# One compact body per engine for the expert loop, with full tiles of 128 slots only

## The reference

```python
def moe_swiglu(h, w_router, w_gu, w_down):
    logits = (h @ w_router).astype(jnp.float32)
    top_vals, top_idx = lax.top_k(logits, TOP_K)          # TOP_K = 2
    gates = jax.nn.softmax(top_vals, axis=-1)
    comb = jnp.sum(jax.nn.one_hot(top_idx, N_EXPERTS, dtype=jnp.float32) * gates[..., None], axis=-2)
    y = jnp.zeros_like(h)
    for e in range(N_EXPERTS):                            # N_EXPERTS = 8
        y = y + comb[..., e:e + 1] * swiglu(h, w_gu[e], w_down[e])
    return y
```

## Time and profile before

| | before |
|---|---|
| median of 3 runs | 1827.52 us (1825.49 to 1830.34) |
| span of the profiled execution | 1824.5 us |
| PE busy | 1688.0 us (93%) |
| DVE busy | 1270.3 us (70%) |
| ACT busy | 1020.9 us (56%) |
| mean granted TensorE clock | 0.964 |
| HBM read | 449.06 MB |

### The profile page before, as it was taken

One profiled execution on the slowest core, in us unless ns is written; L12 is line 12 of the kernel. 1 busy time (PEld: TensorE's weight loads), 2 busy tenths in 40 slices (PEclk: granted clock), 3 DMA queues, 4 the chain that ended last, 5 costly groups with the idle time before them and its releaser, 6 DMA issues.

```text
span 1824.5 us, 21578 instructions
## 1 busy us (share of the span) xinstructions
PE 1688.0 (93%) x7605; PEld 1391.9 (76%) x7606; DVE 1270.3 (70%) x1081; ACT 1020.9 (56%) x883; POOL 9.6 (1%) x22
## 2 busy tenths in 40 slices
PE   7999999999997889979979979979998899799996
PEld 5887778887786778868868868868886688688785
DVE  6645644454697568868878878856654788788886
ACT  4344433433476367757757757644544577577674
POOL 0000000000000000000000000000000000000000
PEclk9999999999998799989989989989998999899999
DMA  9553455555421269979979979946665699799893
GB/s 350 193 199 111 143 189 194 185 192 180 167 96 44 79 230 370 348 252 369 350 254 369 349 255 374 333 164 228 223 215 177 222 378 340 257 368 349 318 367 135
DMA packets 191716, 452.27 MB, mean 248 GB/s; under 512 B 8492, under 2 KB 8892, under 8 KB 191420
## 3 DMA queue, kind: packets, MB, share of 16 engines
q1 hardware_dynamic: 189212, 445.35, 69.2%
q10 hardware_dynamic: 2336, 4.78, 0.7%
HBM read 449.06 MB, written 1.05 MB: 247 GB/s over the span
## 4 chain that ended last, share of the span: by engine, by line
PE 88%; DVE 7%; issue 3%; ACT 1%; DMA 0%; DVEq 0%; POOL 0%; SPq 0%; ACTq 0%; POOLq 0%
PE bank L1218 28%; PE bank L1219 28%; PE bank L1222 26%; DVE y L996 2%; DVE wlo L739 2%; PE bank L1374 2%; PE bank L1483 1%; PE bank L1484 1%; DMA raw<-in_ret_w_in 0%; DVE z L751 0%; PE bank L1464 0%; PE bank L1262 0%; ACT whi L414 0%; DVE res L1160 0%; PE bank L1442 0%
## 5 line engine op out<-in xcount | busy, mean ns | idle before, releaser
L739 DVE TENSOR_TENSOR wlo<-raw,whi 128x2048 fp32r<-128x2048 f32 x422 | 964.3, 2290 | 340.4 <-ACT whi L414 340.1
L414 ACT ACTIVATE whi<-raw 128x2048 fp32r<-128x2048 f32 x422 | 807.7, 1916 | 423.0 <-PE bank L1222 366.3
L1218 PE MATMUL bank<-whi,xh 128*128 128x512 f32 x1520 | 607.9, 400 | 83.4 <-issue 62.4
L1219 PE MATMUL bank<-wlo,xh 128*128 128x512 f32 x1520 | 601.0, 395 | 0.0
L1222 PE MATMUL bank<-whi,xl 128*128 128x512 f32 x1408 | 556.5, 395 | 0.0
L1218 PEld LDWEIGHTS bank<-whi,xh 128*128 128x128 f32 x1520 | 291.8, 192 | 146.6 <-issue 71.1
L1219 PEld LDWEIGHTS bank<-wlo,xh 128*128 128x128 f32 x1520 | 291.3, 192 | 59.1
L1222 PEld LDWEIGHTS bank<-whi,xl 128*128 128x128 f32 x1408 | 269.8, 192 | 57.7
L1218 PE MATMUL bank<-whi,hTh 128*128 128x512 f32 x616 | 242.3, 393 | 4.4 <-DVE hTl L921 2.5
L1219 PE MATMUL bank<-wlo,hTh 128*128 128x512 f32 x616 | 242.6, 394 | 0.0
L1222 PE MATMUL bank<-whi,hTl 128*128 128x512 f32 x560 | 218.6, 390 | 0.0
(11 more groups left out here) (184 smaller groups left out, 792.1 us busy)
## 6 DMA issues: line engine op xcount, KB each, us to landing
raw<-in_moe_w_gu SPq DMA_DIRECT2D x224, 1024.0 KB, 6.4
raw<-in_moe_w_down SPq DMA_DIRECT2D x112, 1024.0 KB, 6.6
raw<-in_ffn_w_gu SPq DMA_DIRECT2D x28, 1024.0 KB, 5.1
raw<-in_ret_w_in SPq DMA_DIRECT2D x24, 1024.0 KB, 6.0
raw<-in_ffn_w_down SPq DMA_DIRECT2D x14, 1024.0 KB, 4.9
raw<-in_conv_w_pw SPq DMA_DIRECT2D x12, 1024.0 KB, 5.0
raw<-in_ret_w_out SPq DMA_DIRECT2D x8, 1024.0 KB, 4.8
res<-in_x SPq DMA_DIRECT2D x2, 512.0 KB, 4.6
```

The costliest lines, as they stand in the source:

```text
L414: nc.scalar.activation(whi[base % SPLIT][:, :], raw[base % RAW][:, :], ACT.Copy).then_inc(hi_done, 1)
L739: nc.vector.tensor_tensor(wlo[base % SPLIT][:, :], raw[base % RAW][:, :], whi[base % SPLIT][:, :].bitcast(f32), ALU.subtract).then_inc(lo_ ...
L1218: nc.tensor.matmul(dst, ah, bh, start=start, stop=False)
L1219: last = nc.tensor.matmul(dst, ah, bl, start=False, stop=stop and al is None)
```

## The change

- `by_need` and its three variants go. On each engine one loop over all eight experts holds one branch: a count above 128 runs `expert(e, (FULL, FULL))` with 24 matmuls a block, all others `expert(e, (FULL,))` with 12. A kind HALF_FULL is defined and not used.
- The gather is per tile of 128 slots. Tile 0 of the next expert is gathered ahead of the last two down blocks; tile 1 at the start of a wide expert.
- The scatter of the previous expert comes after the next expert's two gate blocks. For expert 0 it scatters a column of `comb` that is zero; one more `y_hi`, `y_lo`, scatter and `accumulate` follow the loop. A wide expert scatters its second tile at its own end (`scatter(1, SCAT2)`, `accumulate2`) and PE waits for that.
- The up blocks of an expert's first step are followed by the index transposes, by matmuls with a zero matrix that open the DOWN banks (two, or four for a wide expert), and by the turn. `rows` of an expert then never starts a bank.
- `build_onehot` makes eight writes of 64 columns instead of six, right behind the first `hidden` of an expert. Slot tables take eight small operations instead of two and two.
- xh and xl, and hTh and hTl, lie interleaved in one buffer each. SP loads the blocks in plain order.

The core of the diff:

```diff
-        def by_need(eng, need, piece):
-            with eng.If(need > 0):
-                with eng.If(need > 1):
-                    piece(TWO)
-                with eng.Else():
-                    piece(PACKED)
-            with eng.Else():
-                piece(ONE)
...
# SP
+            with sp.Fori(0, NE) as e:
+                wg, wd = expert(moe_w_gu, e), expert(moe_w_down, e)
+                gu(wg, B_MOE, 0, STEPS * e)
                 with sp.Fori(0, STEPS - 1) as i:
-                    gu(wg, B_MOE + 4, i + 1, STEPS * j + i)
-                    down(wd, B_MOE + 8, i, STEPS * j + i)
+                    gu(wg, B_MOE + 4, i + 1, STEPS * e + i)
+                    down(wd, B_MOE + 8, i, STEPS * e + i)
+                down(wd, B_MOE + 40, STEPS - 1, STEPS * e)
...
# ACT
+            def expert(e, tiles):
+                six, done = STEPS * e, STEPS * e + STEPS
+                xh_gathered(e)
+                if tiles == 2:
+                    xh_gathered2(wide_before(act, e))
+                hi(B_MOE + 1, six)
+                y_hi(B_MOE + 6 * six)
+                hi(B_MOE + 2, six)
+                hi(B_MOE + 3, six)
+                silu(done, B_MOE + 2 + 6 * six, tiles)
+                hi(B_MOE + 4, six)
+                hi(B_MOE + 5, six)
+                ohT_evac(e, tiles)
+                with act.Fori(0, STEPS - 1) as i:
+                    hTh_evac(done + 1 + i, tiles)
+                    hi(B_MOE + 6, six + i)
+                    hi(B_MOE + 7, six + i)
+                    hi(B_MOE + 8, six + i)
+                    silu(done + 1 + i, B_MOE + 6 + 6 * (six + i), tiles)
+                    hi(B_MOE + 9, six + i)
+                    hi(B_MOE + 10, six + i)
+                    hi(B_MOE + 11, six + i)
+                hTh_evac(done + STEPS, tiles)
+                if tiles == 2:
+                    y_hi2(B_MOE + MOE_BLOCKS + 6 * six)
...
# DVE
             def build_onehot(e):
-                for i, (a, b) in enumerate(((0, P), (0, HALF), (HALF, P))):
-                    at_ = (0, P, P)[i]
-                    for t in range(TILES):
-                        last = nc.vector.tensor_scalar(onehot[:, t, at_ + a:at_ + b], iota[:, a:b],
-                                                       slot[:, i, t, bass.ds(e, 1)], None, ALU.is_equal)
+                for h in range(2):
+                    for n in range(2 * TILES):
+                        at_ = n % 2 * P + h * HALF
+                        last = nc.vector.tensor_scalar(onehot[:, n // 2, at_:at_ + HALF], iota[:, h * HALF:(h + 1) * HALF],
+                                                       slot[:, bass.ds(e, 1), n, h], None, ALU.is_equal)
                 last.then_inc(onehot_done, 1)
...
+            def expert(e, tiles):
+                six, done = STEPS * e, STEPS * e + STEPS
+                n2 = wide_before(dve, e) if tiles == 2 else None
+                xl_gathered(e, tiles, n2)
+                lo(B_MOE + 1, six)
+                y_lo(e)
+                lo(B_MOE + 2, six)
+                lo(B_MOE + 3, six)
+                accumulate(e)
+                hidden(done, B_MOE + 4 + 6 * six, tiles)
                 dve.wait_ge(ohT_ps, e + 1)
                 build_onehot(e + 1)
...
                 lo(B_MOE + 4, six)
                 lo(B_MOE + 5, six)
+                with dve.Fori(0, STEPS - 1) as i:
+                    hTl_evac(done + 1 + i, tiles)
+                    for b in range(6, 10):
+                        lo(B_MOE + b, six + i)
+                    hidden(done + 1 + i, B_MOE + 8 + 6 * (six + i), tiles)
+                    lo(B_MOE + 10, six + i)
+                    lo(B_MOE + 11, six + i)
+                hTl_evac(done + STEPS, tiles)
+                if tiles == 2:
+                    y_lo2(n2)
+                    accumulate2(e, n2)
...
# PE
+            def gather(e, tile):
+                for c in range(DC):
+                    dst = bank[2 * tile + c // 4][:, c % 4 * P:(c % 4 + 1) * P]
                     for t in range(TILES):
+                        where = onehot[:, t, tile * P:(tile + 1) * P]
+                        nc.tensor.matmul(dst, zh[:, t, c * P:(c + 1) * P], where, start=t == 0, stop=False)
+                        last = nc.tensor.matmul(dst, zl[:, t, c * P:(c + 1) * P], where, start=False, stop=t == TILES - 1)
+                return last
...
+            def expert(e, kinds):
+                six, done, tiles = STEPS * e, STEPS * e + STEPS, len(kinds)
+                gates = (FULL,) * tiles
+                n2 = wide_before(pe, e) if tiles == 2 else None
+                if tiles == 2:
+                    gather(e, 1).then_inc(gather2_ps, 1)
+                pe.wait_ge(xel_done, e + 1)
+                columns(B_MOE, bank[0:2], 0, kinds=gates, six=six)
+                columns(B_MOE + 1, bank[0:2], 1, kinds=gates, six=six)
+                pe.wait_ge(yl_done, e + 1)
+                scatter(0, SCAT).then_inc(scat_ps, 1)
+                pe.wait_ge(hTl_done, done)
+                columns(B_MOE + 2, bank[2:4], 0, kinds=kinds, six=six)
+                columns(B_MOE + 3, bank[2:4], 1, kinds=kinds, six=six)
+                pe.wait_ge(res_done, 2 * e + 8)
+                onehot_turn(tiles)
+                for n in range(2):
+                    nc.tensor.matmul(DOWN[0][n][:, :], zeros[:, 0:P], zeros[:, :], start=True, stop=False)
+                if tiles == 2:
+                    pe.wait_ge(ohT_done, e + 1)
+                    for n in range(2):
+                        nc.tensor.matmul(DOWN[1][n][:, :], zeros[:, 0:P], zeros[:, :], start=True, stop=False)
+                hT_turn(done, kinds)
+                with pe.Fori(0, STEPS - 1) as i:
+                    pe.wait_ge(silu_done, done + 1 + i)
+                    columns(B_MOE + 4, bank[0:2], 0, kinds=gates, six=six + i)
+                    columns(B_MOE + 5, bank[0:2], 1, kinds=gates, six=six + i)
+                    pe.wait_ge(hTl_done, done + 1 + i)
+                    columns(B_MOE + 6, bank[2:4], 0, kinds=kinds, six=six + i)
+                    columns(B_MOE + 7, bank[2:4], 1, kinds=kinds, six=six + i)
+                    expert_rows(B_MOE + 8, 0, False, kinds, six + i)
+                    expert_rows(B_MOE + 9, 2, False, kinds, six + i)
+                    hT_turn(done + 1 + i, kinds)
+                pe.wait_ge(silu_done, done + STEPS)
+                pe.wait_ge(onehot_done, e + 2)
+                gather(e, 0).then_inc(gather_ps, 1)
+                pe.wait_ge(hTl_done, done + STEPS)
+                expert_rows(B_MOE + 40, 0, False, kinds, six)
+                expert_rows(B_MOE + 41, 2, True, kinds, six)
+                if tiles == 2:
+                    pe.wait_ge(y2l_done, n2 + 1)
+                    scatter(1, SCAT2).then_inc(scat2_ps, 1)
+                    pe.wait_ge(acc2_done, n2 + 1)
...
+            with pe.Fori(0, NE) as e:
+                need = need_of(pe, e)
+                with pe.If(need > 1):
+                    expert(e, (FULL, FULL))
+                with pe.Else():
+                    expert(e, (FULL,))
+            pe.wait_ge(yl_done, NE + 1)
+            scatter(0, SCAT).then_inc(scat_ps, 1)
```

More of the change, by code:

```diff
@@ L501, in silu @@
                     act.wait_ge(hid_done, s)
[L502 to L507, removed]
+                for t in range(tiles):
+                    last = nc.scalar.activation(sgate[:, t, :], bank[t][:, :], ACT.Silu)
@@ L526, in step @@
[L526 to L531, removed]
+                for t in range(tiles):
+                    last = nc.scalar.activation(hTh[:, :, t, :],
+                                                bank[2 + t][:, :].rearrange("p (c n) -> p c n", c=4), ACT.Copy)
+                last.then_inc(hTh_done, 1)
+            def step(base, s, six):
+                hi(base, six)
+                hi(base + 1, six)
+                hTh_evac(s, TILES)
@@ L724, in _ @@
+            act.wait_ge(plan_done, 1)
+            with act.Fori(0, NE) as e:
+                need = need_of(act, e)
+                with act.If(need > 1):
+                    expert(e, 2)
+                with act.Else():
+                    expert(e, 1)
+                with act.If(e < NE - 1):
+                    hi(B_MOE + MOE_BLOCKS, STEPS * e)
+            y_hi(B_MOE + MOE_BLOCKS * NE)
             squares(4)
@@ L1212, in _ @@
+            y_lo(NE)
+            accumulate(NE)
             norm(4)
@@ L1512, in gates @@
-            def gates(base, need, e, s, six=0):
-                def piece(half, tiles):
-                    pe.wait_ge(silu_done, s)
-                    pe.wait_ge(xel_done, 2 * e + half + 1)
-                    columns(base + half, bank[0:2], half, tiles=tiles, six=six)
-                by_need(pe, need, lambda tiles: piece(0, tiles))
-                by_need(pe, need, lambda tiles: piece(1, tiles))
-            def ups(base, need, six=0):
-                for half in range(2):
```

(17 more changed lines are left out.)

535 lines of the change are left out of this document (191 added, 344 removed).

## The result

The changed kernel took 1837.57 us (median of 4 runs, 1835.4 to 1839.02) beside 1826.51 us of the kernel before: 1.0053 of its time, interval 1.0039 to 1.0068. It is slower by half a per cent. (With a fourth run, the median of the kernel before is 1826.51, where the three runs listed ahead had 1827.52.) The forecast was faster by 0.27%, so its sign was wrong, though the time lies inside the range, and just inside the 1810 to 1838 that the forecast gave for free jumps.

What follows compares the result with a forecast made beforehand. PE, busy 93%, bounds the kernel, with code-fetch pauses at seams. Seven experts at 128.5, expert 4 at 265.3 and edges of 12.1 make 1176.9 against 1182.0 us: about 1822.5 us (-0.27%), range 1809 to 1890.

Steps and rivals of the forecast that it cites:

- free jumps: PE's loop and branch jumps at expert seams no longer wait for code; 60%, with its own range 1810 to 1838.
- What a steady step costs: PE's steps at a matmul pitch of 0.2277 us: 16.83 us with one tile, 33.67 with two.
- a new pause comes at the first step: In an expert's first step PE waits for block 4's split, queued on DVE behind hid and build_onehot: 3.35 us.
- Eight one-hot writes: DVE's build_onehot in an expert's first step takes 1.5 us, or 2.0 if each write costs its whole 0.25.
- Clock: ... I take 0.8: Slow matmuls behind a one-tile expert's first-step pauses cost 0.8 us, bounds 0 and 1.8; expert 4 has 2.0.
- the edge at the start: Before the first gates: slot operations and onehot writes +1.2, gather 3.2, its evacuation 2.9 us, all on the path.
- Gather 3.2: A gather of one tile, 32 matmuls of 128 columns on PE, takes 3.2 us (1.9 to 3.8).
- A gather matmul of 128 columns: Its pitch on PE was taken as 0.10 us, between bounds 0.06 and 0.12.
- At the end of expert 4: After its second scatter PE waits for accumulate2 (3.2 us), then the next expert's lo(0) and xl (3.6); seam 0.4.
- Seam 0.4: Between two experts, with code at hand, PE's loop jump, load of need and branch cost 0.4 us (0 to 1.0).
- The lost packing: Expert 4 takes 24 products per block, not 20: 5.5 us more a step, 38 in all.
- The rule cited against the change: Skill text: prefetch is purely sequential, and taken branches outside the two-page window stall, so PE's seam jumps might still cost.

Runs made afterwards that it cites:

- the quarter fill: The changed kernel with 3 zero matmuls, not 11, behind each expert's first turn, in PE's pause for the split of block 4: 1831.93 us, 1.0018.
- the far jump: The changed kernel with 1000 never-run matmuls in PE's wide branch, between the loop's head and the one-tile branch: 1839.00 us, 1.0059.
- the packed kernel: The changed kernel with block 4 split ahead of the hidden product on DVE, and expert 4 packed by HALF_FULL: 1791.55 us, 0.9803 of the kernel before.

## Why the prediction was wrong, step by step

**Right.** That the jumps become free (60%): 23 pages for 92, and no "issue" pause at one-tile seams. What a steady step costs: 16.85 measured for 16.83, 33.65 for 33.67 at two tiles. That a new pause comes at the first step, released by the split L739 (L691 now), behind the one-hot writes: 3.1 us from start to start of its neighbours for 3.35, and the wait for the hidden product 0.2 for 0.5. Eight one-hot writes took 1.38 for 1.5. The period from 793.43 to 921.07, in which no matmul was slow, is 127.64 us; the forecast without its clock term is 127.7.

**Wrong: the step "Clock: ... I take 0.8".** The mechanism was there and its size was wrong. The sum had 7.6 us of slow matmuls in the whole expert stage (seven times 0.8 and 2.0 for expert 4). Measured are 88 x 0.2 = 17.6: +10. Of these +3.6 are in the first steps of the seven one-tile experts (46 slow matmuls, 1.3 us an expert for 0.8), +4.2 in expert 4 (31, 6.2 us for 2.0), and +2.2 at the first gates of the stage (11), for which the sum had nothing. Two things went wrong in it. Its upper bound of 1.8 was taken from one window, with nine matmuls at the low clock; here up to 13 followed a pause (2.6 us). And the rows of pauses that left the clock up were read as a border, which the quarter fill showed not to exist. With the right size the forecast is about 1832, slower than before, so this one term turned its sign. That it is a cost of its own, and not beside another wait, the filled pause shows: 10 us by eleven matmuls per expert that compute nothing. Why one pause is followed by none and the next, as long, by thirteen, no run here shows.

**Wrong: the edge at the start.** "Gather 3.2" was priced at full clock. It ran at 0.50 and took 6.9, 0.21 us a matmul. The first gather of the kernel before has the same 0.21 in its trace (matmuls that start at 633.19, 633.41 and 633.62), so this could have been read; with the shorter wait behind the gather, the step came to 9.2 for 6.1: +3.

**Smaller.** A gather matmul of 128 columns has a pitch of 0.113, not 0.10: +3 over the eight others. The matmul behind the first one of a pause starts 0.33 to 0.59 us later, not 0.23: +2.5 over eleven pauses. At the end of expert 4 the pause was 8.4 by starts for 7.2 forecast: +1.2; a cold jump ended it, and without that jump the forecast's terms there (accumulate2, split, xl) come to 6.6. "Seam 0.4" was 0: -3. First-step pause a little shorter: -3. That these two nearly undo the +5.5 above them is luck. With the clock and the start this accounts for some 14 of the 16.3 us between 1819.4 and 1835.7; the remainder isn't resolved.

**Confirmed in size.** The lost packing: forecast 38, measured 37 in the steps, but the kernel before loses 6.5 at the seam into its PACKED body, so that packing as a whole was worth 31.3 to it. The forecast had taken no such gain at that seam. The seams did bring what the forecast counted, 137 to about 129 us a period; it went to the lost packing and to expert 4's waits, and the clock made it a loss.

**The rule cited against the change.** The Trainium skill, Runtime: NRT & Kernel Launch, section Instruction fetch mechanics, says that a taken branch outside the current two-page window stalls. This case's trace disagrees for PE: back-jumps over 588 matmuls, and over 1588 with the skipped code, cost nothing; the changed kernel fetched one page of PE's code from 665 to 1050, over three seams. Where code had not been touched lately the stall is there: PE's sequencer sat 3.8 us in the jump to the first expert's body and 3.6 in that out of the wide body, and 5.0 and 6.2 in the jumps into the wide body with the far jump and in the packed kernel.

## What to carry to other kernels

Price a pause of PE as the pause plus what the clock takes behind it (0 to 2.6 us here, 1.3 on average over the eight first-step pauses), and don't read a border out of a few that cost nothing. If a pause can't be removed, zero matmuls in it took 10 us off here; better, and worth 30 us here, look at the order on the engine that releases it, for work that could have been done before it. For code, the length of a loop's body decided nothing here; count what an iteration touches. And where the profile names an engine for a wait, look whether PE's sequencer was in a branch: for the 11.1 us before PACKED and the 8.6 us in the packed kernel it was.

## What the runs showed of the hardware

- Whether a jump of PE waits for code doesn't go by its distance: 23 pages for the whole run with a loop body of 588 and of 1588 matmuls alike, against 92 where each iteration wandered over three variants of every piece.
- A jump to code that isn't at hand held PE's sequencer for 3.3 to 4.0 us where one page arrived, and for 6.0 to 6.4 where two did (kernel before); two jumps forward over a body that isn't run took 5.0 and 6.2 us with one page.
- A pause of one length (2.8 us idle) is followed by 0, 7 or 12 to 13 matmuls at 1.2 GHz, at places with the same work ahead of them; 2.1 us of idle time by 7 or none; and one of 2.5 us, behind `yl`, by none in the changed kernel and by six where the first-step pauses were filled.
- Matmuls with zeros can raise the clock: at the start of the stage eight of them at the low level were followed by a gather at 2.4 GHz, which ran at 1.2 GHz without them.
